# First feed-forward's gate and up products with seven block products for eight, on one Trainium2 core

## The chip, the cores and the metric

The program runs on one core of one Trainium2 chip. The metric is the device time of one execution in microseconds (us). The kernel before takes 1785.22 us, the median of three runs (1783.51 to 1785.93).

## What is computed

A block of two layers acts on 512 latent tokens and 256 context tokens of width 1024. Each layer normalizes and modulates its input, mixes the tokens (layer 0: neighbourhood attention and a convolution; layer 1: an mLSTM), and then runs a gated feed-forward of hidden width 2816. Layer 0 does this for all 768 tokens, layer 1 for the 512 latent ones only. The part that matters here:

```python
def swiglu(h, w_gate, w_up, w_down):
    return (jax.nn.silu(h @ w_gate) * (h @ w_up)) @ w_down
...
x = x + g2 * swiglu(modulate(x, norm_ffn_g[l], sh2, sc2), ffn_w_gate[l], ffn_w_up[l], ffn_w_down[l])
if not last:
    ctx = ctx + cg1 * out_ctx
    ctx = ctx + cg2 * swiglu(modulate(ctx, norm_ffn_g[l], csh2, csc2), ffn_w_gate[l], ffn_w_up[l], ffn_w_down[l])
```

The modulation vectors of both layers are products of a conditioning vector with a large matrix (`ada_w`, 96 tiles of 128 columns); 48 of these tiles, those of layer 1, are computed inside the first feed-forward.

## The kernel before

Activations lie feature-major: `X`, `h_hi` and `h_lo` are 128 partitions x 8 tiles x 768 tokens. To keep fp32 accuracy at the pace of the faster fp32r format, each operand is split in two parts, a high part (rounded to fp32r, by a copy on ScalarE) and a low part (the rest, by a subtraction on VectorE). A product of weights and activations is then three matmuls per tile of the contraction: high x high, high x low, low x high.

**One weight chunk** is a row of `in_w`: 128 partitions x 1024 numbers, that is 8 contraction tiles for 128 output features. SyncE loads it into `raw[j]` (j is 0 or 1, its loop is at L377 to L383), as soon as VectorE has finished with the chunk that lay there. ScalarE copies it to `w_hi[j]` (`split_hi`, L452), which waits until the product that last used `w_hi[j]` is done; VectorE subtracts to `w_lo[j]` (`split_lo`, L457). `product` (L471) runs on TensorE:

```python
for w, m in ((w_hi, m_hi), (w_hi, m_lo), (w_lo, m_hi)):
    n += 1
    for a, b in cols:
        last = nc.tensor.matmul(G[j][:, a:b], w[:, j, k], m[:, k, a:b], ...)
```

In the first feed-forward `cols` is `BOTH`, so each weight tile is used by a matmul of 512 columns and one of 256; in the second it is `ONLY`, 512 columns. `G[0]` is PSUM banks 0 and 1, `G[1]` banks 2 and 3.

**The feed-forward** takes its 22 hidden tiles in `GROUPS` of 8, 8 and 6 (the third item of the pair is the count). For each tile a gate product goes to `G[0]` and an up product to `G[1]`. ScalarE applies SiLU to the gate (L607, to `sg`), VectorE multiplies with the up product (L1162, to `ftmp`), ScalarE copies to `c_hi` (L610), VectorE subtracts to `c_lo` (L1164). After a group come eight down products, one for each tile of the 1024 output features, over the 8 or 6 hidden tiles of the group; their last contraction tile waits for the last hidden tile. VectorE adds each into `X` (`residual`, L1150, two instructions of 512 and 256 columns). The first pair of products is written so that each contraction tile is used as soon as the norm has made it (L1716).

**Conditioning tiles.** Between the down products of the first feed-forward stands one round of conditioning work for every two down products, 12 rounds of 4 tiles. ScalarE issues four transfers of 512 KB each (L618), TensorE multiplies them after the even down product (L1725, 64 recorded matmuls a round), ScalarE copies the rows (L622), TensorE folds them after the odd one (L1732), VectorE adds the bias (L1171). In the last group each `residual` is followed by the squares for the next norm (L578, L1105).

The order on each engine is the order in which it is written; all engines run their own in-order queue and wait on semaphores. GpSimd only makes attention masks in layer 0 (L413 to L418) and small products in layer 1 (L443); it is idle during both feed-forwards.

## Time and profile before

| | before |
|---|---|
| median of three runs | 1785.22 us |
| the profiled execution's own time | 1781.29 us |
| its span, first to last instruction | 1779.5 us |
| TensorE busy | 1694.7 us, 95% of the span |
| VectorE busy | 802.9 us, 45% |
| ScalarE busy | 592.7 us, 33% |
| GpSimd busy | 68.0 us, 4% |
| granted TensorE clock, mean | 0.983 |
| first feed-forward | about 444 to 1038 us |
| second feed-forward | about 1405 to 1771 us |

The profile is one execution, recorded by the hardware. An engine's busy time counts its instructions, and matmuls overlap in it, so that the pace of TensorE is read from how often something repeats rather than from one matmul's length. An instruction that others wait for is named as the releaser of their idle time. The granted clock of TensorE is 1.00 at 2.4 GHz and 0.50 at 1.2 GHz.

### The profile page before, as it was taken

To read this page: it belongs to the slowest core of one execution; us is meant where nothing else is said; L and a number is where in the kernel's file an instruction comes from. 1 tells how busy PE (TensorE), PEld (TensorE's weight loads), DVE (VectorE), ACT (ScalarE), POOL (GpSimd) and SP (SyncE) were. 2 spreads that over 40 slices of the span, in tenths; PEclk is the share of its full clock that TensorE was granted. 3 is DMA by queue.
4 is the path that set the end of the run, shared out by engine and by line. 5 is a ranking of instruction groups with operands and counts; after the bars stand their busy time and mean duration, and the time that the engine had idled before them with its cause. 6 is when DMAs were issued, how large, how long until landed. Compare 5 with 4: busy or idle time off the path is not lost.

```text
span 1779.5 us, 26603 instructions
## 1 busy us (share of the span) xinstructions
PE 1694.7 (95%) x10524; PEld 1404.3 (79%) x10524; DVE 802.9 (45%) x1192; ACT 592.7 (33%) x1021; POOL 68.0 (4%) x116
## 2 busy tenths in 40 slices
PE   5999999888999999999999988999998899999998
PEld 4888877677888888888888866777776688888886
DVE  5787776534422222222222355666644533333333
ACT  4344444442322112221122232455564422222221
POOL 0321011000000000000000000000000000000000
PEclk9999999899999999999999998999999999999999
DMA  8713333211112532124212531111113232233223
GB/s 333 108 48 120 128 110 119 82 34 62 48 59 63 197 106 59 61 97 165 102 60 91 183 130 39 46 36 36 48 48 107 71 105 95 94 94 106 94 95 118
DMA packets 47219, 168.99 MB, mean 95 GB/s; under 512 B 5296, under 2 KB 5552, under 8 KB 47024
## 3 DMA queue, kind: packets, MB, share of 16 engines
q1 hardware_dynamic: 31408, 115.47, 20.1%
q10 hardware_dynamic: 14976, 51.52, 7.9%
q0 software_dynamic: 768, 1.08, 0.8%
...
## 4 chain that ended last, share of the span: by engine, by line
PE 89%; DVE 3%; ACT 3%; DMA 2%; issue 1%; SPq 0%; ACTq 0%; DVEq 0%
PE PS L471 53%; PE PS L1839 9%; PE PS L2027 7%; PE PS L1716 3%; DMA scr<-in_ada 2%; PE PS L1725 2%; PE PS L1882 2%; PE PS L1898 1%; PE PS L2115 1%; PE PS L1732 1%; PE PS L2114 1%; DVE c_early L1466 1%; PE PS L1778 1%; PE PS L1864 1%; PE PS L1982 1%
## 5 line engine op out<-in xcount | busy, mean ns | idle before, releaser
L457 DVE TENSOR_TENSOR w_lo<-raw,w_hi 128x1024 fp32r<-128x1024 f32 x196 | 239.8, 1224 | 253.2 <-ACT w_hi L452 247.3
L471 PE MATMUL PS<-h_hi,w_hi 128*128 128x512 f32 x1008 | 302.2, 354 | 2.5 <-DVE w_lo L457 2.5
L471 PE MATMUL PS<-h_hi,w_lo 128*128 128x512 f32 x1008 | 301.8, 353 | 0.0
L471 PE MATMUL PS<-h_lo,w_hi 128*128 128x512 f32 x1008 | 301.8, 353 | 0.0
L452 ACT ACTIVATE w_hi<-raw 128x1024 fp32r<-128x1024 f32 x196 | 206.5, 1054 | 261.3 <-PE PS L471 217.9
L471 PE MATMUL PS<-c_hi,w_hi 128*128 128x512 f32 (+1 forms) x672 | 203.5, 357 | 4.7 <-DVE w_lo L457 4.7
L471 PE MATMUL PS<-c_lo,w_hi 128*128 128x512 f32 (+1 forms) x672 | 201.5, 354 | 0.0
L471 PE MATMUL PS<-c_hi,w_lo 128*128 128x512 f32 (+1 forms) x672 | 201.4, 354 | 0.0
L471 PEld LDWEIGHTS PS<-h_hi,w_hi 128*128 128x128 f32 x1008 | 165.1, 188 | 30.5 <-DVE w_lo L457 3.3
L471 PEld LDWEIGHTS PS<-h_hi,w_lo 128*128 128x128 f32 x1008 | 165.2, 188 | 27.5
L471 PEld LDWEIGHTS PS<-h_lo,w_hi 128*128 128x128 f32 x1008 | 165.2, 188 | 27.5
L1150 DVE SCALAR_TENSOR_TENSOR X<-PS,mod,X 128x512 f32 (+1 forms) x96 | 60.6, 659 | 256.3 <-PE PS L471 240.1
L471 PEld LDWEIGHTS PS<-c_hi,w_hi 128*128 128x128 f32 x672 | 109.9, 188 | 25.5 <-DVE w_lo L457 5.6
L1284 DVE SCALAR_TENSOR_TENSOR c_early<-X,small,c_early 128x798 f32<-128x798 f32 x120 | 126.0, 1050 | 2.9
L471 PEld LDWEIGHTS PS<-c_hi,w_lo 128*128 128x128 f32 x672 | 110.2, 188 | 18.7
L471 PEld LDWEIGHTS PS<-c_lo,w_hi 128*128 128x128 f32 x672 | 110.1, 188 | 18.4
L610 ACT ACTIVATE c_hi<-scr 128x768 f32 (+3 forms) x44 | 32.6, 742 | 266.5 <-DVE scr L1162 266.5
L1162 DVE TENSOR_TENSOR scr<-PS,scr 128x768 f32<-128x768 f32 (+1 forms) x44 | 36.3, 825 | 169.6 <-PE PS L471 169.6
L2027 PE MATMUL PS<-h_hi,w_hi 128*128 128x512 f32 (+1 forms) x264 | 85.5, 378 | 12.8 <-ACT c_early L944 9.4
L607 ACT ACTIVATE scr<-PS 128x768 f32<-128x768 f32 (+1 forms) x44 | 31.1, 707 | 190.4 <-PE PS L471 184.6
L2027 PE MATMUL PS<-h_hi,w_lo 128*128 128x512 f32 (+1 forms) x264 | 81.0, 361 | 0.0
L2027 PE MATMUL PS<-h_lo,w_hi 128*128 128x512 f32 (+1 forms) x264 | 80.6, 360 | 0.0
...
## 6 DMA issues: line engine op xcount, KB each, us to landing
raw<-in_w SPq DMA_DIRECT2D x196, 512.0 KB, 3.5
...
scr<-in_ada SPq DMA_DIRECT2D x4, 1024.0 KB, 14.6
...
```

The lines of the kernel that those rows point to most:

```text
L452: nc.scalar.activation(w_hi[:, j], raw[:, j].rearrange("p (k n) -> p k n", k=KT), ACT.Copy).then_inc(s_hi, 1)
L457: nc.vector.tensor_tensor(w_lo[:, j], raw[:, j].rearrange("p (k n) -> p k n", k=KT), w_hi[:, j].bitcast(f32), ALU.subtract).then_inc(s_lo, 1)
L471: last = nc.tensor.matmul(G[j][:, a:b], w[:, j, k], m[:, k, a:b], start=(n == 1), stop=(n == 3 * k_tiles))
L610: nc.scalar.activation(c_hi[:, bass.ds(i, 1), 0:cols].rearrange("p a n -> p (a n)"), ftmp[:, 0:cols], ACT.Copy).then_inc(s_hhi, 1)
L1150: i = V.scalar_tensor_tensor(out=xs, in0=G[j][:, a:b], scalar=gv, in1=xs, op0=ALU.mult, op1=ALU.add)
L1162: V.tensor_tensor(ftmp[:, 0:cols], G[1][:, 0:cols], sg[:, 0:cols], ALU.mult).then_inc(s_gf[1], 1)
L1284: V.scalar_tensor_tensor(out=y, in0=src, scalar=w, in1=y, op0=ALU.mult, op1=ALU.add)\
L1716: last = MM(G[j][:, a:b], x[:, j, k], m[:, k, a:b], start=(k == 0 and n == 0), stop=(k == KT - 1 and n == 2))
L1725: last = MM(PS[g:g + 32, bank, 128 * q:128 * q + 128], sT[:, k], w[:, 128 * k:128 * k + 128], start=(k < 4), stop=(k >= 4))
L1839: last = MM(dst[:, a:b], w[:, p % 2, k], m[:, k, a:b], start=(k == 0 and n == 0), stop=(k == KT - 1 and n == 2))
L1882: last = MM(PS[0:size, 6 + h, 128 * n:128 * n + 128], Pb[:, U % 2, h, c:c + size], dg[:, U % 2, h], start=True, stop=True)
L2027: last = MM(dst[:, a:b], w[:, i % 2, k], m[:, k, a:b], start=(k == 0 and n == 0), stop=(k == KT - 1 and n == 2))
```

## The change

**The block product.** In the first feed-forward, 20 of the 22 hidden tiles are no longer computed by a gate and an up product over 768 tokens. The weights of a pair (gate tile and up tile) and the activations are cut in two halves of the contraction (4 tiles each) and the tokens in two halves of 384 (`HALF`). Of the 2 x 2 block product, Strassen's scheme (in Winograd's form) needs seven products of blocks in place of eight: `block(q, b)` for pair `q`, `b` from 0 to 6, each of 4 contraction tiles x 3 matmuls of 384 columns, into PSUM bank `BLOCK_BANK[b]`. The first two hidden tiles (`PLAIN`) stay as they were.

**Weight sums.** With a0, a1 the two halves of the gate tile and u0, u1 those of the up tile, blocks 1, 4, 2 and 6 take a0 - u0, u0 + u1, u0 + u1 - a0 and a1 - (u0 + u1 - a0). GpSimd makes them (`weight_sum`, four 128 x 512 operations a pair), mostly in place in the loaded chunks. Each block's weights are then split as before, now in pieces of 512 numbers (`block_hi` on ScalarE, `block_lo` on VectorE), into five slots: the four halves of `w_hi`/`w_lo` and `slot4`. Slots 2 and 3 are used twice a pair (`BLOCK_SLOT`).

**Activation sums.** Once, at the start: GpSimd and VectorE add high and low parts of the four blocks of `h` back together (`whole`, two each, 128 x 1536), VectorE forms four differences (`h_sum`), ScalarE and VectorE split them (`sum_hi`, `sum_lo`, four each). One of them is put over a part of `h_hi`/`h_lo`, and waits for the last plain product to have read it (`s_b12`).

**After the blocks.** ScalarE copies block 0's result to SBUF (`p1s`), VectorE forms seven sums of PSUM blocks with 384-column intermediates (`sums`, `gate0`, `up1`, `up0`, `gate1`); SiLU and the multiplication with it are each done in two halves; `c_hi` and `c_lo` are made as before.

**Groups.** `GROUPS` is 6, 6, 6 and 4 hidden tiles, in both feed-forwards, so that there are 32 down products in each instead of 24, over the same 22 hidden tiles. The conditioning work of the first feed-forward is 16 rounds of 3 tiles. Both weight buffers `raw` and `adaw` carry the gate and up chunks of alternate pairs, and conditioning tiles go to `adaw` and a piece of `scr`. The code of the first feed-forward is written out (`ffn_first`) where there were loops; the second (`ffn`) keeps its loops.

```diff
 GD_END = 20
-GROUPS = ((0, 8), (8, 8), (16, 6))
+GROUPS = ((0, 6), (6, 6), (12, 6), (18, 4))
+PLAIN = 2
+PAIRS = tuple(f0 + nf - PLAIN for f0, nf in GROUPS)
+FIRST = (0,) + PAIRS[:-1]
 GRID = 64
...
+        SUMS = [[tw[:, x, y] for y in range(2)] for x in range(2)] + [[h_hi[:, 0:4, HALF:T], h_lo[:, 0:4, HALF:T]]]
+        SUMS += [[v[:, 6:8].rearrange("p a (b n) -> p (a b) n", b=2) for v in (c_hi, c_lo)]]
+        SUM_RAW = (four(tw_raw[:, 0, 1]), four(tw_raw[:, 1, 1]), b12, four(c_early[:, 1, 6 * T:8 * T]))
+        B11, B21, B22 = ([x[:, a:a + 4, b:b + HALF] for x in (h_hi, h_lo)] for a, b in ((0, 0), (4, 0), (4, HALF)))
+        MOVING = (B11, SUMS[2], SUMS[1], B21, SUMS[0], SUMS[3], B22)
+        SLOTS = [[x[:, j, a:a + 4] for x in (w_hi, w_lo)] for j in range(2) for a in (0, 4)]
+        SLOTS += [[slot4[:, 0], slot4[:, 1]]]
+        BLOCK_SLOT = (0, 1, 2, 3, 4, 2, 3)
+        BLOCK_BANK = (0, 1, 2, 3, 5, 6, 7)
...
+        def slot_free(engine, q, b):
+            g = FIRST.index(q) if q in FIRST else None
+            if b >= 5:
+                engine.wait_ge(s_bp, 7 * q + b - 2)
+            elif g is None:
+                engine.wait_ge(s_bp, 7 * (q - 1) + (1, 2, 6, 7, 5)[b])
+            elif b < 4:
+                engine.wait_ge(s_gemm, R_F0 + 2 * PLAIN + 8 * g - (b < 2))
+            else:
+                engine.wait_ge(s_adm, 48 + 12 * g)
...
+            R = R_F0 + 2 * PLAIN
+            for g in range(len(GROUPS)):
+                for q in range(FIRST[g], PAIRS[g]):
+                    for c in range(2):
+                        if q == FIRST[g]:
+                            sp.wait_ge(s_lo, R - 1 + c)
+                        elif q == 1:
+                            sp.wait_ge(s_adm, 48)
+                        elif q == FIRST[g] + 1:
+                            sp.wait_ge(s_adm, 48 + 12 * g)
+                        else:
+                            sp.wait_ge(s_bl, 7 * (q - 1))
+                        sp.dma_start(chunk(q, c), A["w"][R + 2 * q + c]).then_inc(s_pw[q % 2][c], 16)
...
+            def weight_sum(q, i):
+                a0, a1, u0, u1 = (four(chunk(q, c)[:, n:n + 512]) for c in range(2) for n in (0, 512))
+                if i == 0:
+                    slot_free(pool, q, 1)
+                    for c in range(2):
+                        pool.wait_ge(s_pw[q % 2][c], 16 * (q // 2) + 16)
+                    dst, x, y, op = block_raw(q, 1), a0, u0, ALU.subtract
+                elif i == 1:
+                    pool.wait_ge(s_sb, 4 * q + 1)
+                    dst, x, y, op = u0, u0, u1, ALU.add
+                elif i == 2:
+                    pool.wait_ge(s_sb, 4 * q + 2)
+                    pool.wait_ge(s_bl, 7 * q + 1)
+                    dst, x, y, op = a0, u0, a0, ALU.subtract
+                else:
+                    pool.wait_ge(s_sb, 4 * q + 3)
+                    pool.wait_ge(s_bl, 7 * q + 4)
+                    dst, x, y, op = a1, a1, a0, ALU.subtract
+                nc.gpsimd.tensor_tensor(dst, x, y, op).then_inc(s_sb, 1)
...
+        def block_hi(act, q, b):
+            slot_free(act, q, b)
+            if b in (0, 3, 5):
+                act.wait_ge(s_pw[q % 2][b == 5], 16 * (q // 2) + 16)
+            else:
+                act.wait_ge(s_sb, 4 * q + {1: 1, 4: 2, 2: 3, 6: 4}[b])
+            nc.scalar.activation(SLOTS[BLOCK_SLOT[b]][0], block_raw(q, b), ACT.Copy).then_inc(s_bh, 1)
+        def block_lo(dve, q, b):
+            hi, lo = SLOTS[BLOCK_SLOT[b]]
+            dve.wait_ge(s_bh, 7 * q + b + 1)
+            nc.vector.tensor_tensor(lo, block_raw(q, b), hi.bitcast(f32), ALU.subtract).then_inc(s_bl, 1)
...
+                        last = q + 1 == PAIRS[g]
+                        block_hi(act, q, 2)
+                        if q > FIRST[g]:
+                            second_half_silu(q - 1)
+                        act.wait_ge(s_bp, 7 * q + 1)
+                        act.wait_ge(s_g0, q)
+                        nc.scalar.activation(p1s, partial(0), ACT.Copy).then_inc(s_sn, 1)
+                        block_hi(act, q, 3)
+                        if q == 0:
+                            act.wait_ge(s_gf[1], half + 1)
+                            hidden_hi(1)
+                        elif q > FIRST[g]:
+                            pair_hi(q - 1, q + 1 - f0)
+                        block_hi(act, q, 4)
+                        block_hi(act, q, 5)
+                        block_hi(act, q, 6)
+                        first_half_silu(q)
+                        if not last:
+                            block_hi(act, q + 1, 0)
+                            block_hi(act, q + 1, 1)
+                    act.wait_ge(s_bp, 7 * q + 2)
+                    split_hi(act, R // 2, 0)
+                    act.wait_ge(s_bl, 7 * q + 7)
+                    act.wait_ge(s_bp, 7 * q + 5)
+                    ada_next(4 * g)
+                    second_half_silu(q)
+                    pair_hi(q, q + 2 - f0)
...
+                def sums(q):
+                    dve.wait_ge(s_bp, 7 * q + 3)
+                    dve.wait_ge(s_sn, q + 1)
+                    dve.wait_ge(s_u4, q)
+                    V.tensor_tensor(u2s, partial(2), p1s, ALU.add).then_inc(s_u2, 1)
+                    dve.wait_ge(s_u2, q + 1)
+                    dve.wait_ge(s_u0, q)
+                    V.tensor_tensor(u3s, partial(1), u2s, ALU.add).then_inc(s_u3, 1)
+                def gate0(q):
+                    dve.wait_ge(s_bp, 7 * q + 4)
+                    if q:
+                        dve.wait_ge(s_f, 2 * q - 1)
+                    else:
+                        dve.wait_ge(s_gf[1], half + 1)
+                    V.tensor_tensor(sg[:, 0:HALF], partial(3), p1s, ALU.add).then_inc(s_g0, 1)
+                def up1(q):
+                    dve.wait_ge(s_bp, 7 * q + 5)
+                    dve.wait_ge(s_g1s, q)
+                    V.tensor_tensor(u4s, partial(4), u2s, ALU.add).then_inc(s_u4, 1)
+                    dve.wait_ge(s_u3, q + 1)
+                    dve.wait_ge(s_hid, q + PLAIN)
+                    V.tensor_tensor(ftmp[:, HALF:T], partial(4), u3s, ALU.add).then_inc(s_u1, 1)
+                def up0(q):
+                    dve.wait_ge(s_bp, 7 * q + 6)
+                    V.tensor_tensor(ftmp[:, 0:HALF], partial(5), u3s, ALU.add).then_inc(s_u0, 1)
...
+                dve.wait_ge(s_h, 16)
+                whole(b12, h_hi[:, 0:4, HALF:T], h_lo[:, 0:4, HALF:T])
+                split_lo(dve, half, 0)
+                whole(b22, *B22)
+                gated(half - 1)
+                dve.wait_ge(s_ty, 1)
+                dve.wait_ge(s_tz, 1)
+                h_sum(SUM_RAW[0], b12, b11)
+                hidden_lo(0, 0)
+                split_lo(dve, half, 1)
+                dve.wait_ge(s_ty, 2)
+                dve.wait_ge(s_ts, 1)
+                h_sum(SUM_RAW[2], b22, b12)
+                h_sum(SUM_RAW[1], b22, SUM_RAW[0])
+                dve.wait_ge(s_tz, 2)
+                dve.wait_ge(s_ts, 3)
+                h_sum(SUM_RAW[3], b21, SUM_RAW[1])
+                block_lo(dve, 0, 0)
+                sum_lo(2)
+                block_lo(dve, 0, 1)
+                sum_lo(1)
+                gated(half)
...
+                        if q > FIRST[g]:
+                            gate1(q - 1)
+                        block_lo(dve, q, 2)
+                        if q > FIRST[g]:
+                            gated1(q - 1)
+                        if q == 0:
+                            sum_lo(0)
+                        block_lo(dve, q, 3)
+                        if q == 0:
+                            hidden_lo(1, 1)
+                            sum_lo(3)
+                        elif q > FIRST[g]:
+                            hidden_lo(q + 1, q + 1 - f0)
+                        block_lo(dve, q, 4)
+                        sums(q)
+                        block_lo(dve, q, 5)
+                        gate0(q)
+                        block_lo(dve, q, 6)
+                        up1(q)
+                        if not last:
+                            block_lo(dve, q + 1, 0)
+                        else:
+                            split_lo(dve, R // 2, 0)
+                        up0(q)
+                        gated0(q)
+                        if not last:
+                            block_lo(dve, q + 1, 1)
+                    gate1(q)
+                    gated1(q)
+                    hidden_lo(q + 2, q + 2 - f0)
...
+            def block(q, b):
+                g = FIRST.index(q) if q in FIRST else None
+                pe.wait_ge(s_bl, 7 * q + b + 1)
+                if q:
+                    pe.wait_ge((s_sn, s_u3, s_u2, s_g0, s_u1, s_u0, s_g1s)[b], q)
+                if g is not None and b in (0, 2):
+                    pe.wait_ge(s_gf[b // 2], R_F0 // 2 + PLAIN + 4 * g)
+                if g and b == 4:
+                    pe.wait_ge(s_mod, 20 + 4 * g)
+                if q == 0 and b in (1, 2, 4, 5):
+                    pe.wait_ge(s_tl[{1: 2, 2: 1, 4: 0, 5: 3}[b]], 1)
+                (w_h, w_l), (m_h, m_l) = SLOTS[BLOCK_SLOT[b]], MOVING[b]
+                for k in range(4):
+                    for n, (x, m) in enumerate(((w_h, m_h), (w_h, m_l), (w_l, m_h))):
+                        last = MM(partial(b), x[:, k], m[:, k], start=(k == 0 and n == 0), stop=(k == 3 and n == 2))
+                last.then_inc(s_bp, 1)
```

**VectorE, one pair of the first feed-forward.** `L457` was `split_lo`; now `L602` is `block_lo`, `L1410` to `L1443` are the sums over PSUM, `L1449` and `L1455` the multiplications with the SiLU, `L1403` makes `c_lo`. Before, the body of the loop:

```order
L457 TENSOR_TENSOR w_lo<-raw,w_hi 128x1024
L456 ISA
L457 TENSOR_TENSOR w_lo<-raw,w_hi 128x1024
L1162 TENSOR_TENSOR scr<-PS,scr 128x768
L1163 REGISTER_ALU
L1164 ISA
L1164 TENSOR_TENSOR c_lo<-scr,c_hi 128x768
```

Now, a pair within a group, from the sums of its first blocks on (the two rows at the end belong to the next pair's block 1 and to the last sum of this one):

```order
L1410 TENSOR_TENSOR scr<-PS,scr 128x384
L1413 TENSOR_TENSOR scr<-PS,scr 128x384
L602 TENSOR_TENSOR w_lo<-raw,w_hi 128x512
L1422 TENSOR_TENSOR scr<-PS,scr 128x384
L602 TENSOR_TENSOR w_lo<-raw,w_hi 128x512
L1428 TENSOR_TENSOR scr<-PS,scr 128x384
L1431 TENSOR_TENSOR scr<-PS,scr 128x384
L602 TENSOR_TENSOR w_lo<-adaw,w_hi 128x512
L1436 TENSOR_TENSOR scr<-PS,scr 128x384
L1449 TENSOR_TENSOR scr<-scr 128x384
L602 TENSOR_TENSOR w_lo<-w_early,w_hi 128x512
L1443 TENSOR_TENSOR scr<-PS,scr 128x384
```

Four operations a pair became 17, the weight parts of the next block standing between the sums of the last.

**VectorE, between the norm and the first block.** `L586` is now `split_lo`, `L1398` the plain multiplication, `L1388` an `h_sum`, `L1393` a `sum_lo`. Before, only `split_lo`, L1162 and L1164 stood there. Now, from the first plain multiplication to the low part of block 1:

```order
L1398 TENSOR_TENSOR scr<-PS,scr 128x768
L1388 TENSOR_TENSOR scr<-c_early 128x1536
L1403 TENSOR_TENSOR c_lo<-scr,c_hi 128x768
L586 TENSOR_TENSOR w_lo<-raw,w_hi 128x1024
L1388 TENSOR_TENSOR c_early<-c_early 128x1536
L1388 TENSOR_TENSOR scr<-c_early,scr 128x1536
L1388 TENSOR_TENSOR c_early<-c_early,scr 128x1536
L602 TENSOR_TENSOR w_lo<-raw,w_hi 128x512
L1393 TENSOR_TENSOR h_lo<-c_early,h_hi 128x4x384
L602 TENSOR_TENSOR w_lo<-w_early,w_hi 128x512
```

Six operations of 1536 elements stand here that were not there before.

**GpSimd.** Before, no instruction stood between the last mask of layer 0 and layer 1. Now:

```order
L518 AFFINE_SELECT c_early<-X 128x64
L527 TENSOR_TENSOR c_early<-h_hi,h_lo 128x1536 x2
L548 TENSOR_TENSOR w_early<-raw 128x512
L548 TENSOR_TENSOR raw<-raw 128x512 x3
L548 TENSOR_TENSOR w_early<-adaw 128x512
L548 TENSOR_TENSOR adaw<-adaw 128x512 x3
```

The last four rows repeat ten times, for 20 pairs.

## Rows read from the trace of the kernel before

**Rows 1.** The page's parts 1 and 2: busy share of each engine, and the granted clock
```profile
PE 1694.7 (95%) x10524; PEld 1404.3 (79%) x10524; DVE 802.9 (45%) x1192; ACT 592.7 (33%) x1021; POOL 68.0 (4%) x116
...
PEclk9999999899999999999999998999999999999999
```

**Rows 2.** Windows of TensorE: stretch, its length, PE busy (xinstructions), granted clock, DMA share, GB/s
```profile
478.00:981.00 503.00, 501.60 (x3369) 1.00 0.28 98
```

**Rows 3.** Timeline of VectorE, first feed-forward (start, us, engine, line, operation, idle before)
```profile
481.63 0.96 DVE L1162 TENSOR_TENSOR scr<-PS,scr 128x768 f32<-128x768 f32 x1 [5.37 <-PE PS L471]
...
581.48 0.96 DVE L1162 TENSOR_TENSOR scr<-PS,scr 128x768 f32<-128x768 f32 x1 [5.37 <-PE PS L471]
```

**Rows 4.** Timeline of VectorE, second feed-forward
```profile
1433.69 0.69 DVE L1162 TENSOR_TENSOR scr<-PS,scr 128x512 f32<-128x512 f32 x1 [2.71 <-PE PS L471]
...
1498.97 0.69 DVE L1162 TENSOR_TENSOR scr<-PS,scr 128x512 f32<-128x512 f32 x1 [2.70 <-PE PS L471]
```

**Rows 5.** Timeline of TensorE inside one product: matmuls of 512 and 256 columns, weight loads
```profile
584.21 0.31 PEld L471 LDWEIGHTS PS<-c_hi,w_hi 128*128 128x128 f32 x2
584.32 0.51 PE L471 MATMUL PS<-c_hi,w_hi 128*128 128x512 f32 x2
```

**Rows 6.** Groups by line and form, VectorE and ScalarE: xcount, busy us, mean ns of one
```profile
L457 DVE TENSOR_TENSOR w_lo<-raw,w_hi 128x1024 fp32r<-128x1024 f32 x196 | 239.8, 1224 | 253.2 <-ACT w_hi L452 247.3
...
L1162 DVE TENSOR_TENSOR scr<-PS,scr 128x768 f32<-128x768 f32 x22 | 21.1, 958 | 112.8 <-PE PS L471 112.8
...
L1162 DVE TENSOR_TENSOR scr<-PS,scr 128x512 f32<-128x512 f32 x22 | 15.2, 692 | 56.8 <-PE PS L471 56.8
...
L610 ACT ACTIVATE c_hi<-scr 128x768 f32 x21 | 17.8, 849 | 162.0 <-DVE scr L1162 162.0
...
L610 ACT ACTIVATE c_hi<-scr 128x512 f32 x21 | 13.3, 634 | 100.4 <-DVE scr L1162 100.4
```

**Rows 7.** Groups by line and form, GpSimd
```profile
L443 POOL TENSOR_TENSOR scr<-scr,const 48x512 f32<-48x512 f32 x16 | 16.7, 1042 | 227.2 <-PE PS L2099 198.7 <-DVE scr L1618 28.6
```

**Rows 8.** Timeline of VectorE and GpSimd, first mixer; then one line of VectorE: ns min/median/max
```profile
155.55 1.22 DVE L457 TENSOR_TENSOR w_lo<-raw,w_hi 128x1024 fp32r<-128x1024 f32 x1
155.58 1.33 POOL L415 TENSOR_SCALAR_AFFINE_SELECT scr<-X 128x64 f32<-128x64 f32 x1 [51.85 <-DVE scr L1318]
...
L1284 DVE SCALAR_TENSOR_TENSOR c_early<-X,small,c_early x120: 1035/1050/1087, 62.1 to 305.6; 128x798 f32<-128x798 f32 x120
```

**Rows 9.** Timeline of VectorE, then TensorE, where the first feed-forward begins
```profile
457.53 0.48 DVE L1118 SCALAR_TENSOR_TENSOR h_lo<-scr,mod,h_hi 128x256 fp32r<-128x256 f32 x1
...
463.33 1.23 DVE L457 TENSOR_TENSOR w_lo<-raw,w_hi 128x1024 fp32r<-128x1024 f32 x1 [5.33 <-ACT w_hi L452]
...
464.62 0.61 PE L471 MATMUL PS<-h_hi,w_hi 128*128 128x512 f32 x2 [0.99 <-DVE w_lo L457]
```

**Rows 10.** Timeline of TensorE after a long idle, and the window behind it
```profile
444.17 0.98 PE L1716 MATMUL PS<-h_hi,w_hi 128*128 128x512 f32 x2 [5.54 <-DVE h_lo L1118]
...
444.00:449.00 5.00, 4.83 (x15) 0.50 0.00 0
```

**Rows 11.** Timeline of VectorE and TensorE, down products; what TensorE waited for before L1725
```profile
600.52 1.14 DVE L1150 SCALAR_TENSOR_TENSOR X<-PS,mod,X 128x512 f32 x2 [8.27 <-PE PS L471]
...
620.14 1.14 DVE L1150 SCALAR_TENSOR_TENSOR X<-PS,mod,X 128x512 f32 x2 [8.13 <-PE PS L471]
...
589.62 1.95 PE L1725 MATMUL PS<-scr,sT 128*32 128x128 f32 x64
...
  DMA scr<-in_ada: 8.2, 13
```

**Rows 12.** Timeline of VectorE, last group of the second feed-forward, and its weight transfers
```profile
1738.33 0.69 DVE L1162 TENSOR_TENSOR scr<-PS,scr 128x512 f32<-128x512 f32 x1 [2.70 <-PE PS L471]
1739.93 0.69 DVE L1164 TENSOR_TENSOR c_lo<-scr,c_hi 128x512 f32 x1 [0.91 <-ACT c_hi L610]
...
DMA to landing us min/median/max: 3.4/3.5/3.6
```

410 lines of the change are left out of this document (276 added, 134 removed).

## The prediction

> **What bounds the kernel now.** I read the page's busy shares first. TensorE is busy 95% of the span at a granted clock near 1.0, every other engine under half [rows 1]. In the window that holds nearly all of the first feed-forward, 503.0 us long, TensorE has work for 501.60 us at a granted clock of 1.00 [rows 2]. So in this stage no wait ends last: only fewer or shorter matmuls can shorten it, provided that the others keep up.
>
> The pace comes from a repeat. From one plain multiplication of a pair to the next but five lie six periods, 99.85 us, so a pair (48 times 512 + 256 columns) takes 16.64 us [rows 3]. In the second feed-forward six periods take 65.28 us, so 48 matmuls of 512 columns take 10.88 us, 226.7 ns each [rows 4]. The remaining 16.64 - 10.88 = 5.76 us are 48 matmuls of 256 columns, 120.0 ns each. The difference, 106.7 ns for 256 columns, is 2.4 GHz; a matmul costs its columns plus 13.3 ns.
>
> **What the change removes.** By that line a matmul of 384 columns takes 160.0 + 13.3 = 173.3 ns. A pair of the new kind has 7 x 4 x 3 = 84 of them: 14.56 us. Against 16.64 us this is 2.08 us less, and for 20 pairs **-41.6 us**. The interpolation rests on the weight load staying hidden. One load is recorded as 188 ns or so (two take 0.31 us, starting 0.12 us apart), but the 512-column matmul behind it starts 0.11 us after the load [rows 5], and a 256-column matmul leaves it only 120 ns. 173 ns is more room than that.
>
> **What the other engines must now do in 14.56 us.** VectorE's 128x512 and 128x768 operations take 0.692 and 0.958 us, so 1.04 ns an element, and 0.559 us for 384. ScalarE's take 0.634 and 0.849 us, and 0.527 us for 384 [rows 6]. A pair needs on VectorE 7 low parts (4.84), 7 sums and 2 multiplications (5.03) and one `c_lo` (0.96): 10.8 us. On ScalarE 7 high parts (4.44), one copy and two SiLUs (1.58), one `c_hi` (0.85): 6.9 us. GpSimd needs four sums; the nearest row is its 48x512 operation of 1.042 us [rows 7], so 4.2 us.
>
> Totals below 14.56 are not enough: each block needs its weights in time. I walk VectorE's queue from the start of block 0, 2.08 us a block, with 0.25 us from a block's end to its reader and 0.1 us for a handover (my readings). The two sums after block 2 (end 6.24) are done at 7.7, the low part for block 5 at 8.4; it is due at 10.40. `gate0` after block 3, then block 6's low part at 9.9; due 12.48. `up1`, then the next block 0's at 12.5; due 14.56. `up0`, the multiplication, then the next block 1's at 14.6; due 16.64. `gate1`, then block 2's at 16.1; due 18.72. Block 3's high part stands behind ScalarE's copy of block 0: low part 18.8, due 20.80. `c_lo` and block 4's: 20.6, due 22.88. **The spare is never under 2.0 us.** The PSUM banks are read a whole pair ahead. The chunk for a pair is asked for when the pair two before it is split, some 9 us ahead of the first sum of it; a transfer takes 3.5 us [rows 12]. I cost all this at nothing, with 1.5 us in total for stalls of single blocks; its cover is those 2.0 us.
>
> **GpSimd against VectorE.** One thing can use up the spare. A GpSimd operation on 64 columns that started 0.03 us after a `w_lo` lasted 1.33 us, to just behind VectorE's end. VectorE's own accumulations next to GpSimd's masks stayed between 1035 and 1087 ns in 120 cases [rows 8]. So GpSimd waits for VectorE; whether VectorE waits for GpSimd the trace does not show, since GpSimd's masks are short. Bounds: 0, or four times 1.042 us a pair. I take a value between, since both do not meet each time and sums that read PSUM ran beside GpSimd. VectorE then has 10.8 to 15.0 us of work, likely about 13, under 14.56.
>
> The Trainium skill ("SBUF — State Buffer", section "SBUF: two separate sides") says the pair of ports that VectorE and GpSimd share is an exclusive lock, taken for a whole instruction when VectorE has two SBUF inputs and GpSimd reads SBUF, and that the second to start blocks. By that rule the trace agrees for GpSimd waiting; VectorE waiting would be my first rival below.
>
> **The start.** The last `h_lo` ends at 458.0 us; TensorE's second pair waited for its first low part until 464.6 [rows 9]. New before that low part: one 1536-element operation on VectorE (0.958 + 768 x 1.04 ns = 1.76 us) and two on GpSimd (3 x 1.042 = 3.1 us each at most). If all three stand in line, the part is ready at 458.0 + 1.8 + 6.3 + 1.2 = 467.3, 2.7 us late; if GpSimd never holds VectorE, nothing is late. Then VectorE has 1.76 us nine times more (one `whole`, four `h_sum`, four `sum_lo`), 15.8 us, besides its usual work, until the first pair's middle, 25 us later. In my walk the low part for block 4 of pair 0 comes about 1 us late, and with GpSimd's first sums between 3 us late. A wait also can cost clock: after 5.54 us idle, TensorE ran 4.83 us at 0.50 of its clock [rows 10], 2.4 us lost. Bounds 0 and 9 us; I take **+5**, the middle, since all the queues are crowded there.
>
> **More rounds and groups.** Two down products with a round take 620.14 - 600.52 = 19.62 us, against 16.64 without: 2.98 us a round, 35.8 us for 12. Of this 1.95 us are 64 row matmuls [rows 11], for three tiles 0.27 + 47 x 0.0267 = 1.5 us; the rest scaled gives about 0.8. So 16 x 2.35 = 37.6 us: **+2**. Bounds: 16 rounds at three quarters, 0; 16 unshortened rounds, +11.9. TensorE waited 8.2 us for conditioning transfers [rows 11], mostly in the last group, where ScalarE asks for them behind the squares. There products shrink from 6.24 to 4.16 us, but only three rounds instead of four wait, for three tiles instead of four: I take no change, bounds -4 and +4.
>
> A group's last hidden tile must be ready before the last contraction tile of its first down product. Its path is now 0.25 + 0.56 + 0.53 + 0.56 + 0.85 + 0.96 us and four handovers, 4.1 us. With six tiles that matmul starts 5.2 us after the blocks: covered by the five tiles ahead. With four it starts at 9 x 0.3467 = 3.1 us: **+1**. In the second feed-forward `c_lo` ends 1740.62, 2.5 us after the up product (the multiplication at 1738.33 began 0.25 us behind it) [rows 12], against 9 x 0.2267 = 2.0 us: +0.5. There a weight chunk also is the longer cycle in the group of four: transfer 3.5, high 1.05, low 1.23, handovers 0.25, 6.0 us for two products that take 5.44; three times over, +1.7. Together **+2.2**. The eight more evictions and splits of each feed-forward are covered elsewhere, since six tiles give products of 6.24 and 4.08 us against 1.23 + 1.1 us of VectorE. The code is written out where it looped; the mixers run written-out code now at the same pace, so nothing.
>
> **Sum.** -41.6 + 1.5 + 5 + 2 + 0 + 1 + 2.2 = -29.9 us. Against the profiled execution's 1781.29 us this gives 1751.4; that run stood 3.9 us below the median of the three runs, 1785.22, against which I predict **1755.3 us**. Within this case the ends give about 1746 to 1769.
>
> **Rivals.** (1) GpSimd holds VectorE for each whole sum. VectorE's pair is then 10.8 + 4.2 = 15.0 us, up to 15.8 with gaps that its waits for blocks leave, and it sets the pace: 20 x 0.44 to 20 x 1.24, +9 to +25 us, about 1772. For it: the 1.33 us row shows that one engine can wait for the other's instruction. Against: it would need nearly every sum to collide. Chance 0.13.
>
> (2) Slower: GpSimd's sums on 128 partitions with two plain inputs are much longer than the 48-partition row, and hold VectorE. The gain of 41.6 less 11.7 of costs leaves 29.9 us, 1.5 us a pair, so the change loses once a pair passes 16.1 us; with VectorE at 10.8 + 4s this is s = 1.3 us. At twice the row, 2.08 us, a pair takes 19.2 us, +92 us: about 1848. Against: the operation works on partitions side by side, and the row's 512 elements are the same. Chance 0.06.
>
> (3) The weight load does set the pace, because a single matmul of 384 columns now stands behind each load: 84 x 0.188 = 15.8 us a pair, +24.6 us, about 1780. Against: the 256-column matmuls at 120 ns. Chance 0.04.
>
> The forecast has 0.77. Range, with the start and GpSimd wide: **1746 to 1776**. A measurement here can tell about 0.2%, 3.6 us. Faster by more than that 0.90, within it 0.03, slower 0.07: the forecast and nearly all of (1) and (3) are faster, (2) and a tail of (1) are not.
>
> **What would show it.** TensorE's blocks at 173 ns a matmul and 14.56 us from one `gate0` to the next, with next to no wait for `block_lo`. GpSimd's sums near 1.04 us, longer only where they start inside a VectorE instruction. VectorE's 512-element low parts at 0.69 us; at up to 1.7 us they would show (1). A wait of TensorE of a few microseconds near the second plain pair and in pair 0. In the last groups, short waits before the last contraction tile. I am wrong if a pair's period is over 15 us, or if the start costs over 9 us.

## The result, and the profile after

The changed kernel takes 1762.16 us (median of 4 runs, 1759.95 to 1766.52), beside 1785.58 us (4 runs, 1783.51 to 1787.18) for the kernel before: ratio 0.9876, 95% interval 0.9854 to 0.9898. The prediction was 1755.3 us, range 1746 to 1776. The profiled execution took 1763.85 us with a span of 1761.7 us, 17.8 us under the span of before.

The page, busy time by engine and granted clock by slice (compare [rows 1]):

```profile
PE 1666.7 (95%) x10284; PEld 1410.9 (80%) x10284; DVE 1008.5 (57%) x1506; ACT 668.3 (38%) x1185; POOL 211.7 (12%) x198
...
PEclk8999999999999999999999988999999999999999
```

TensorE still sets the time. It is busy 28 us less and the span is only 17.8 us shorter, so some 10 us of new idle time must be somewhere. I cut the span where TensorE's rows change their operands (the first row of a stage to the first row of the next); the last column is the difference.

| stretch | before, us | after, us | difference |
|---|---|---|---|
| last plain pair ahead of the first block | one pair, 16.65 | 18.09 | +1.4 |
| 20 pairs | 20 of 21 pairs in 349.72: 333.1 | 65.26 + 87.76 + 87.76 + 58.54 = 299.3 | -33.8 |
| down stages of the first feed-forward | 78.58 + 78.41 + 75.43 = 232.4 | 3 x 59.92 + 60.93 = 240.7 | +8.3 |
| mixer to second feed-forward | 361.2 | 364.4 | +3.2 |
| second feed-forward | 363.0 | 366.2 | +3.2 |

The five differences add up to -17.7; the rest of the execution is the same to 0.2 us. Windows of the changed kernel (stretch, length, busy us of PE, PEld, DVE, ACT and POOL with instructions, granted clock, DMA share, GB/s): the groups' pairs, then a down stage and the last one.

```profile
482.57:547.83 65.26, 61.08 (x339) 59.91 (x337) 54.06 (x71) 24.28 (x42) 24.99 (x14) 0.97 0.19 65
607.75:695.51 87.76, 87.76 (x507) 87.76 (x507) 67.65 (x101) 35.61 (x63) 33.99 (x21) 1.00 0.21 72
...
903.11:961.65 58.54, 58.54 (x338) 58.54 (x338) 44.26 (x67) 23.17 (x41) 20.73 (x13) 1.00 0.20 72
547.83:607.75 59.92, 59.92 (x505) 51.66 (x505) 21.29 (x30) 12.19 (x16) 4.53 (x3) 1.00 0.50 176
...
961.65:1015.42 53.77, 47.68 (x413) 38.45 (x412) 28.02 (x39) 20.66 (x25) 0.00 (x0) 0.97 0.56 190
```

Six pairs take 87.76 us, 14.63 us each, 84 matmuls of 174.1 ns; TensorE has no gap in them. The first four need 65.26 us, 6.7 us more than four times 14.63, with 4.2 us of TensorE's time idle. VectorE has 67.65 / 6 = 11.3 us a pair, GpSimd 5.7, ScalarE 5.9. Of the 6.7 us, 4.2 are waits for VectorE, and most of the rest is a lower granted clock behind the longest of them. The timeline of TensorE (the first two rows belong to the plain pair ahead, the others to pair 0):

```profile
464.48 0.61 PE L615 MATMUL PS<-h_hi,w_hi 128*128 128x512 f32 x2 [1.12 <-DVE w_lo L586]
...
473.99 0.61 PE L615 MATMUL PS<-h_hi,w_hi 128*128 128x512 f32 x2 [0.92 <-DVE w_lo L586]
...
485.37 0.44 PE L2112 MATMUL PS<-h_hi,w_hi 128*128 128x384 f32 x1 [0.52 <-DVE w_lo L602]
...
488.51 0.62 PE L2112 MATMUL PS<-h_sums,w_hi 128*128 128x384 f32 x2 [0.75 <-DVE w_lo L602]
...
496.08 3.63 PE L2112 MATMUL PS<-h_sums,slot 128*128 128x384 f32 x12 [2.91 <-DVE slot L602]
```

Behind the wait of 2.91 us, 12 matmuls take 3.63 us where 12 x 0.174 = 2.1 would do, at a granted clock of 0.60 (window, columns as above):

```profile
496.08:500.37 4.29, 4.29 (x16) 4.29 (x17) 3.29 (x7) 1.56 (x3) 1.09 (x1) 0.60 0.13 23
```

The timelines of VectorE and GpSimd over the same time show what VectorE was doing:

```profile
464.34 5.06 DVE L1384 TENSOR_TENSOR c_early<-h_hi,h_lo 128x1536 f32<-128x1536 f32 x1
...
480.77 2.85 DVE L1393 TENSOR_TENSOR h_lo<-c_early,h_hi 128x1536 fp32r<-128x1536 f32 x1
...
491.51 2.84 DVE L1393 TENSOR_TENSOR c_lo<-c_early,c_hi 128x1536 fp32r<-128x1536 f32 x1
...
494.28 1.75 DVE L602 TENSOR_TENSOR slot<-raw,slot 128x512 fp32r<-128x512 f32 x1
```

```profile
458.24 9.54 POOL L527 TENSOR_TENSOR c_early<-h_hi,h_lo 128x1536 f32<-128x1536 f32 x2 [153.49 <-DVE h_lo L1342]
...
490.87 1.88 POOL L548 TENSOR_TENSOR raw<-raw 128x512 f32<-128x512 f32 x1 [6.10 <-DVE w_lo L602]
```

Other operations on 1536 elements take VectorE 1.75 us, low parts of 512 elements 0.69 us. The longest ends its own length behind the end of a GpSimd operation: at 464.34 + 5.06 = 469.40, beside 458.24 + 9.54 = 467.78 and 1.75 us of its own; so does the one at 491.51, beside GpSimd's end at 492.75. (From the first plain multiplication to block 1's low part stand five operations of 1536 elements, not six as the section on the change counts.) The same holds inside the pairs. VectorE's groups by form from 607.75 to 695.5 us (xcount, busy us, mean ns, idle before):

```profile
L602 DVE TENSOR_TENSOR w_lo<-adaw,w_hi 128x512 fp32r<-128x512 f32 x15 | 10.8, 720 | 4.6 <-ACT w_hi L596 4.3
L602 DVE TENSOR_TENSOR slot<-adaw,slot 128x512 fp32r<-128x512 f32 x3 | 5.4, 1784 | 0.0
...
L602 DVE TENSOR_TENSOR slot<-raw,slot 128x512 fp32r<-128x512 f32 x3 | 4.2, 1417 | 0.0
...
L1449 DVE TENSOR_TENSOR scr<-scr 128x384 f32<-128x384 f32 x6 | 4.2, 699 | 0.6
...
L1410 DVE TENSOR_TENSOR scr<-PS,scr 128x384 f32<-128x384 f32 x6 | 3.3, 547 | 1.9 <-PE PS L2112 1.9
```

The low part of block 4 always meets the next pair's weight sum and takes 1.4 to 1.8 us; sums that read PSUM keep 0.55 us. GpSimd's sums take 1.6 us in the mean, not 1.04:

```profile
L548 POOL TENSOR_TENSOR adaw<-adaw 128x512 f32<-128x512 f32 x9 | 14.5, 1606 | 25.1 <-DVE w_lo L602 24.9
L548 POOL TENSOR_TENSOR raw<-raw 128x512 f32<-128x512 f32 x7 | 11.5, 1638 | 23.9 <-DVE w_lo L602 23.7
```

In the last down stage TensorE waits for conditioning transfers. Waits of TensorE from 440 to 1100 us (total us, times, longest):

```profile
PE PS L2087 <- DMA adaw<-in_ada: 2.7, 5, 1.0
PE PS L2087 <- DMA scr<-in_ada: 2.6, 3, 1.2
```

That is 5.3 us, all in the last down stage, beside 3.0 us in the kernel before.

### The profile page after: what moved, and what is told of

It reads as the page before. It is cut to its first block, busy times and chain, and to the rows that moved or that the text cites. A ratio compares the mean times of both kernels' runs of the same rounds, so it can differ in the third digit from the quotient of the medians.

```text
span 1761.7 us, 26390 instructions
## 1 busy us (share of the span) xinstructions
PE 1666.7 (95%) x10284; PEld 1410.9 (80%) x10284; DVE 1008.5 (57%) x1506; ACT 668.3 (38%) x1185; POOL 211.7 (12%) x198
## 4 chain that ended last, share of the span: by engine, by line
PE 86%; DVE 5%; ACT 4%; DMA 3%; issue 1%; SPq 0%; ACTq 0%; DVEq 0%
PE PS L615 33%; PE PS L2112 16%; PE PS L2235 9%; PE PS L2423 7%; PE PS L2078 3%; PE PS L2087 3%; PE PS L2278 2%; DMA scr<-in_ada 2%; PE PS L2294 1%; PE PS L2511 1%; PE PS L2510 1%; PE PS L2094 1%; PE PS L2378 1%; PE PS L2174 1%; PE PS L2260 1%
## 5 line engine op out<-in xcount | busy, mean ns | idle before, releaser
L586 DVE TENSOR_TENSOR w_lo<-raw,w_hi 128x1024 fp32r<-128x1024 f32 x172 | 210.6, 1225 | 120.3 <-ACT w_hi L581 114.0
L1374 DVE SCALAR_TENSOR_TENSOR X<-PS,mod,X 128x512 f32<-128x512 f32 (+1 forms) x120 | 75.7, 659 | 226.4 <-PE PS L615 210.0
L615 PE MATMUL PS<-h_hi,w_hi 128*128 128x512 f32 x368 | 139.2, 385 | 3.6 <-DVE w_lo L586 3.6
L615 PE MATMUL PS<-h_hi,w_lo 128*128 128x512 f32 x368 | 139.0, 385 | 0.0
L615 PE MATMUL PS<-h_lo,w_hi 128*128 128x512 f32 x368 | 138.9, 384 | 0.0
L2112 PE MATMUL PS<-h_hi,w_hi 128*128 128x384 f32 x320 | 107.5, 336 | 0.5 <-DVE w_lo L602 0.5
L2112 PE MATMUL PS<-h_lo,w_hi 128*128 128x384 f32 x320 | 107.0, 335 | 0.0
L2112 PE MATMUL PS<-h_hi,w_lo 128*128 128x384 f32 x320 | 107.0, 334 | 0.0
L615 PEld LDWEIGHTS PS<-h_hi,w_hi 128*128 128x128 f32 x368 | 68.0, 188 | 18.5 <-DVE w_lo L586 4.6
L615 PEld LDWEIGHTS PS<-h_lo,w_hi 128*128 128x128 f32 x368 | 67.9, 188 | 13.8
L615 PEld LDWEIGHTS PS<-h_hi,w_lo 128*128 128x128 f32 x368 | 68.0, 188 | 13.6
```

The lines of the kernel that those rows point to most:

```text
L586: nc.vector.tensor_tensor(w_lo[:, j], raw[:, j].rearrange("p (k n) -> p k n", k=KT), w_hi[:, j].bitcast(f32), ALU.subtract).then_inc(s_lo, 1)
L1374: i = V.scalar_tensor_tensor(out=xs, in0=G[j][:, a:b], scalar=gv, in1=xs, op0=ALU.mult, op1=ALU.add)
L2112: last = MM(partial(b), x[:, k], m[:, k], start=(k == 0 and n == 0), stop=(k == 3 and n == 2))
```

## The experiments

Theory: the pairs are worth 40 us and TensorE paces them; VectorE and GpSimd exclude each other in both directions, which is hidden behind TensorE in the steady pairs and costs only at the start; the rest of the loss is the regrouping. Rivals: GpSimd's sums hold the pairs up, the down stages are slow because of the block products' traffic, the start is VectorE's own work.

**The regrouping alone.** The kernel before, with

```diff
-GROUPS = ((0, 8), (8, 8), (16, 6))
+GROUPS = ((0, 6), (6, 6), (12, 6), (18, 4))
-                    for q in range(4):      # four conditioning tiles a round, 12 rounds
+                    for q in range(3):      # three, 16 rounds
```

> The kernel before with the regrouping alone: both feed-forwards in groups of 6, 6, 6 and 4 tiles, three conditioning tiles a round in 16 rounds, all products plain, nothing on GpSimd. Theory A (the regrouping costs, the block products give): the rounds of the first feed-forward cost about 4 us more than before, its last down stage about 5 us (transfers of the conditioning weights that the stage of four tiles is too short for), the second feed-forward about 3 us: 12 us in all, 1797.5 us, ratio 1.007, and the block products by themselves give 35 us. Rival B (the down stages are slow because GpSimd's sums and the other transfers of the block products disturb them): the regrouping costs under 4 us, at most 1789.5 us, and the stage of four tiles takes the same 19.6 us per two products as the stage of six tiles before.

Measured: 1806.57 us, ratio 1.0136 (1.0101 to 1.0170), twice what theory A gave. By stages against before: down stages +11.3 us, second feed-forward +3.5 us, mixer +1.5 us, all near theory A but for the first, and **+6.8 us in the plain pairs, whose code is unchanged**. Rival B falls: the regrouping alone costs the down stages more than theory A gave them. In the plain pairs TensorE has no gap and its granted clock is 1.00. Timelines of TensorE, two rows that lie 48 rows apart, first of the kernel before, then of this one:

```profile
465.06 0.52 PE L471 MATMUL PS<-h_lo,w_hi 128*128 128x512 f32 x2
...
481.71 0.51 PE L471 MATMUL PS<-h_lo,w_hi 128*128 128x512 f32 x2
```

```profile
465.06 0.51 PE L471 MATMUL PS<-h_lo,w_hi 128*128 128x512 f32 x2
...
482.01 0.51 PE L471 MATMUL PS<-h_lo,w_hi 128*128 128x512 f32 x2
```

A row is one matmul of 512 and one of 256 columns. They follow each other in 16.65 / 48 = 346.9 ns in the one and 16.95 / 48 = 353.1 ns in the other. In the first feed-forwards of all the traces nearly all uninterrupted stretches of such rows lie at 346.7 or at 353.3 ns (within 1 ns), and nearly all keep their rhythm from one interruption to the next. The kernel before has 346.7 in all its pairs but the first, and 353.3 in five of its 24 down products (96 of 528 rows). This kernel has 353.3 in nearly every stretch: 17.0 us a pair, and in the down products 432 rows more than before x 6.6 ns = 2.9 us.

The changed kernel has 353.3 in its down stages too, from the second product on, in about 370 rows more than the kernel before. So of its +8.3 us there, 2.4 us are this rhythm. A down stage of six tiles takes 59.92 us, of which 18 rows x 0.3467 + 126 x 0.3533 = 50.8 us are the products; 2.29 us are left for each of its four rounds, 36.6 us for 16. In the kernel before the same sum, 78.42 - 192 x 0.3467 = 11.85 us for four rounds, gives 35.5 us for 12. So the rounds cost 1.1 us, and the last stage the other 4.8. This last figure is no fixed one: in this trace and the seven others of kernels with the same last stage, the stage takes 58.8 to 64.2 us. The pairs of matmuls of 384 columns keep 174.1 ns each.

**Is the rhythm drawn anew in each execution?** Two kernels: the first feed-forward alone regrouped, and the kernel before once more.

```diff
-                for g, (f0, nf) in enumerate(GROUPS):
+                for g, (f0, nf) in enumerate((GROUPS, GROUPS1)[layer]):   # GROUPS1: 8, 8, 6
```

> The kernel before with the regrouping of its first feed-forward alone (6, 6, 6 and 4 tiles, three conditioning tiles a round); the second keeps 8, 8 and 6. In the earlier run with both regrouped, TensorE's rows of two matmuls (512 and 256 columns) were 353.3 ns apart from 450 to 1055 us, in the kernel before 346.7 ns, though the code of a pair is the same: that made 6.8 us in the pairs and 3.5 us in the down products. Theory A (regrouping costs 1 us in the rounds and 5 to 6 us in the last down stage, and the rhythm of 353.3 ns comes with it again): 17.0 us a pair, the kernel 20 us over the one before, ratio 1.011. Theory B (the rhythm of a stretch is drawn anew in each execution): stretches at 346.7 and at 353.3 ns mixed, pairs of 16.65 us in some of them, ratio 1.004 to 1.008.

> The kernel before once more, for a second trace of it. Theory A (the rhythm belongs to the kernel): rows of two matmuls 346.7 ns apart in the first feed-forward, pairs of 16.65 us, as in its first trace. Theory B (drawn anew in each execution): some stretches of it at 353.3 ns, pairs there of 16.97 us.

Measured: ratio 1.0098 (1.0077 to 1.0120) and 353.3 ns throughout, six pairs in 101.85 us; the kernel before again 346.7 ns, eight pairs in 133.21 us. Windows of the two, in this order:

```profile
612.24:714.09 101.85, 101.85 (x578) 88.28 (x578) 24.80 (x25) 20.22 (x23) 0.00 (x0) 1.00 0.20 62
```

```profile
658.54:791.75 133.21, 133.21 (x770) 116.50 (x770) 33.16 (x33) 27.10 (x31) 0.00 (x0) 1.00 0.19 63
```

Theory A holds for the first feed-forward's plain pairs: two traces of the kernel before agree, and so do the two regrouped kernels; the second trace of the kernel before differs from the first in which of its down products have 353.3. All ten traces of kernels with block products have 353.3 in the down stages, from the second product of each on, but for short pieces in the last stage. Elsewhere it does change from one execution to the next: the one plain pair before the block products ran at 346.7 up to its wait in the first trace of the changed kernel and at 353.3 in the second. What sets it was not found. Against the regrouped plain kernel (1.0136) the block products are worth 2.6% of the kernel before, 46 us; some 6 of them (960 rows x 6.6 ns) are the slower rhythm in that kernel's 20 pairs.

**The conditioning transfers of the last down stage, issued one product earlier.**

```diff
+                        if g < 3 and o and o % 2 == 0:
-                        if o and o % 2 == 0:
                             ada_next(4 * g + o // 2)
...
                         if g == 3:
+                            if o % 2 and o < 7:
+                                ada_next(4 * g + o // 2 + 1)
```

> The changed kernel with one thing moved: in the last down stage of the first feed-forward ACT issues the next three transfers of conditioning weights right behind the copy that ends a round, one product earlier than now. Theory A (TensorE waits there for these transfers, about 5 us in all): the last down stage falls from 53.6 to about 49 us, 1757.5 us for the kernel, 4 to 5 us under the changed one. Rival B (the transfers share their time with the weight transfers, whose sum is what the stage waits for; earlier issue only moves the wait): under 1 us gained.

Measured: ratio 0.9837 (0.9810 to 0.9864), 1754.00 us beside 1781.45 for before; TensorE's waits for these transfers are gone, and the last down stage with the norm behind it takes 52.72 instead of 60.93 us. Windows of its products alone, of the changed kernel and of this one:

```profile
961.65:1013.30 51.65, 45.71 (x406) 37.36 (x405) 25.95 (x36) 18.76 (x23) 0.00 (x0) 0.97 0.58 197
```

```profile
963.26:1006.70 43.44, 42.89 (x406) 36.53 (x405) 26.12 (x36) 18.09 (x23) 0.00 (x0) 1.00 0.65 224
```

TensorE's idle time falls from 5.9 to 0.6 us, its busy time for the same 406 matmuls by 2.8 us, with the granted clock from 0.97 to 1.00: behind the second round's waits, 12 rows had taken 5.65 us, 471 ns each instead of 353. Theory A holds, and the gain is larger than its 4 to 5 us. Rival B falls, although the transfers did get slower (median 5.7 and 7.1 us to landing, from 4.4 and 5.7): they now have the time.

**The second feed-forward in groups of 8, 8 and 6.**

```diff
-                for g, (f0, nf) in enumerate(GROUPS):
+                for g, (f0, nf) in enumerate(GROUPS1):      # in the second feed-forward: 8, 8, 6
```

> The changed kernel with the second feed-forward back in groups of 8, 8 and 6 tiles, the first as changed. Theory A (one more round of residuals and a last group of only four tiles cost 3 us there): the second feed-forward takes 363.0 us as before instead of 366.2, 1759 us for the kernel. Rival B (its extra time comes from elsewhere, from order or alignment of the transfers after the mixers): under 1 us gained.

Measured: the second feed-forward took 363.1 us, 3.1 us less, as theory A said. The whole is less clear: 0.9868 (0.9836 to 0.9900), which contains the ratio without the edit.

**All four additions of 1536 columns on VectorE.**

```diff
-            for dst, (hi, lo) in ((b11, B11), (b21, B21)):
-                nc.gpsimd.tensor_tensor(dst, hi.bitcast(f32), lo.bitcast(f32), ALU.add).then_inc(s_tz, 1)
                 whole(b12, h_hi[:, 0:4, HALF:T], h_lo[:, 0:4, HALF:T])
+                whole(b11, *B11)
                 split_lo(dve, half, 0)
-                whole(b22, *B22)
                 gated(half - 1)
+                whole(b22, *B22)
...
+                whole(b21, *B21)
```

> The changed kernel with the two additions of 1536 columns that GpSimd does at the start of the first feed-forward (9.54 us for the two) moved to VectorE, where the other two stand; GpSimd then does nothing until the weight sums. Theory A (GpSimd and VectorE exclude each other while both read two operands from SBUF, and VectorE's addition of 5.06 us at 464.34 is one of 1.76 us that waits for GpSimd): all four additions take about 1.8 us each on VectorE, the waits of 2.9 us and less before block (0, 2) and its neighbours shrink, and the start costs 2 to 4 us less than in the changed kernel, 1759 us. Rival B (no exclusion, the 5.06 us are the operation's own reads): VectorE has two more operations of 3.4 us in pair 0, the first blocks wait longer, and the kernel is 2 to 5 us slower than the changed one, 1765 us or more.

Measured: the additions on VectorE take 1.75 us each,

```profile
459.41 3.43 DVE L1380 TENSOR_TENSOR c_early<-h_hi,h_lo 128x1536 f32<-128x1536 f32 x2
...
465.75 1.75 DVE L1380 TENSOR_TENSOR c_early<-h_hi,h_lo 128x1536 f32<-128x1536 f32 x1
```

and from the feed-forward's first row to its first down product it takes 101.1 instead of 103.5 us: -2.4 us, as theory A said of the start. VectorE spends 6.9 us on four of them, as much as on two beside GpSimd (1.76 + 5.06 us): the 3.3 us of the long one were waiting. But the wait of 2.9 us in pair 0 stayed as it was, and the ratio 0.9892 (0.9861 to 0.9922) doesn't tell the kernel from the changed one.

**More, other and less work on GpSimd.** Behind (or instead of) its 80 weight sums:

```diff
                 nc.gpsimd.tensor_tensor(dst, x, y, op).then_inc(s_sb, 1)
+                # first:  one more sum of 128x512, const + const
+                # second: two memsets of 128x512
-                # third:  for i > 0 the sum on [:, :, 0:1] alone
```

> The changed kernel with one more addition of 128x512 on GpSimd behind each of its 80 weight sums (two operands from the constants in SBUF, the result never read). Theory A (VectorE and GpSimd exclude each other while both read SBUF): GpSimd has 8 instead of 4 operations in a pair, VectorE's three low parts with two SBUF operands that meet one grow from 0.69 to 1.4 us and more, VectorE's busy time in six pairs rises from 67.4 us by 6 to 25 us, while the sums that read PSUM keep their 0.55 us; the pair stays at 14.6 us as long as VectorE is under that, at most 15.5 us: 0 to 18 us for the kernel. Rival B (no exclusion, only GpSimd itself is slower beside VectorE): VectorE's durations and the pair's 14.6 us stay as they are.

> The same dose as the one before in another form: behind each weight sum two memsets of 128x512 on GpSimd, which read nothing. Theory A (exclusion by what both read): VectorE's low parts keep their present mix of about 0.7 us and, beside a weight sum, 1.4 to 1.8 us, VectorE's busy time in six pairs stays within 2 us of 67.4, the pair at 14.6 us. Rival B (any GpSimd work beside VectorE costs it): busy time rises as it does with the sums.

> The changed kernel with three of GpSimd's four weight sums of each pair cut to one column in four places (it leaves out their other columns, so the block weights are other ones). Theory A (TensorE's matmuls pace the pair, the exclusion is hidden): the pair stays at 14.6 us, VectorE's low parts that wait for GpSimd now (0.79 to 1.78 us) fall to 0.7 us, VectorE's busy time in six pairs from 67.4 us by 4 to 8 us, the kernel within 0.2% of the changed one outside pair 0. Rival B (the weight sums hold the pairs up in waits too short to be seen): the pair falls by 0.05 us or more, to 14.56 us.

The third leaves out most columns of three of the four sums, so its results are other ones. One execution of each: 1769.36, 1761.39 and 1757.62 us, beside 1780.99 for before. Windows of the first group of six pairs, in this order (compare 607.75 to 695.51 of the changed kernel above):

```profile
609.66:700.01 90.35, 89.30 (x506) 87.42 (x506) 81.24 (x101) 35.58 (x63) 68.80 (x43) 1.00 0.20 70
```

```profile
605.05:692.81 87.76, 87.76 (x506) 87.76 (x506) 69.33 (x101) 35.73 (x63) 53.40 (x63) 1.00 0.20 72
```

```profile
601.46:689.21 87.75, 87.75 (x506) 87.75 (x506) 60.20 (x101) 35.56 (x63) 15.28 (x21) 1.00 0.20 73
```

VectorE does the same operations in all four, in 60.2 us with narrow sums, 67.7 with the kernel's own, 69.3 with memsets added and 81.2 with sums added. So 42 memsets (22.1 us of GpSimd) cost it 1.7 us, 22 added sums 13.6 us, 0.6 us each. By form, with narrow sums and with added sums:

```profile
L603 DVE TENSOR_TENSOR slot<-adaw,slot 128x512 fp32r<-128x512 f32 x3 | 2.1, 690 | 0.0
```

```profile
L608 DVE TENSOR_TENSOR w_lo<-w_early,w_hi 128x512 fp32r<-128x512 f32 x5 | 8.9, 1778 | 0.0
...
L1420 DVE TENSOR_TENSOR scr<-PS,scr 128x384 f32<-128x384 f32 x6 | 3.3, 558 | 0.2
```

VectorE's operations with two SBUF operands wait for GpSimd's, those that read PSUM don't. By "SBUF: two separate sides" of the Trainium skill's "SBUF — State Buffer" an operation blocks while the other engine reads SBUF through the ports they share; that is what the runs show. The same six pairs take 87.76 us with narrow sums and with the kernel's own: the kernel's conflicts are hidden behind TensorE, rival B falls. With added sums they show, 90.35 / 6 = 15.06 us a pair, and over the 20 pairs 14 waits for block 4's low part, four of them in these six.

The narrow sums tell what GpSimd costs at the start: the first four pairs take 60.39 instead of 65.26 us. **4.9 of their 6.7 us are GpSimd's weight sums**, the three of each pair that were cut, by their own length and by what they hold up: the low part of an activation sum at 479.33 there takes 1.75 us where it took 2.85, and so does the one at 487.88. The waits of 0.52 and 0.75 us are gone and the longest is 1.69 us:

```profile
491.36 2.36 PE L2113 MATMUL PS<-h_sums,slot 128*128 128x384 f32 x12 [1.69 <-DVE slot L603]
```

That is 2.5 us of waits. Most of the other half of the 4.9 us is the clock: the 12 matmuls behind this shorter wait take 2.36 us and the granted clock stays at 1.00.

**The order on VectorE in pair 0**, with the changed kernel again beside it.

```diff
                         if q == 0:
                             hidden_lo(1, 1)
-                            sum_lo(3)
...
                         block_lo(dve, q, 4)
+                        if q == 0:
+                            sum_lo(3)
                         sums(q)
```

> The changed kernel again, as it is, beside the two that follow, on their chip: 0.9876 of the kernel before, within its interval of 0.9854 to 0.9898.

> The changed kernel with VectorE's order in pair 0 changed at one place: the low part of activation sum 3, which block 5 is the first to need, stands behind the low part of block 4's weights instead of ahead of it. Theory A (TensorE's wait of 2.91 us there, and the stretch at half clock behind it, come from VectorE's order, not from GpSimd's sum): the wait falls to 1.3 us or less, the 12 matmuls behind it from 3.6 to about 2.3 us, the stretch from the first block to the first down product from 65.3 to about 62.5 us, the kernel 2 to 4 us under the changed one. Rival B (GpSimd's third weight sum ends too late anyway): the wait stays over 2 us. Rival C: block 5 waits instead for its low part, and nothing is won.

Measured on one chip: the changed kernel 0.9869 (0.9849 to 0.9889), this one 0.9867 (0.9845 to 0.9890). The timeline of TensorE in pair 0:

```profile
492.31 2.39 PE L2113 MATMUL PS<-h_sums,slot 128*128 128x384 f32 x12 [0.21 <-DVE slot L602]
...
496.74 0.45 PE L2113 MATMUL PS<-c_hi,w_hi 128*128 128x384 f32 x1 [2.05 <-DVE w_lo L602]
```

Rival C: the wait of 2.91 us went from block 4 to block 5, and the stretch took 64.89 instead of 65.26 us. In the changed kernel VectorE is busy without a gap from 463 to 499 us. This other order only moved the wait; fewer conflicts, with the narrow sums, did shorten it.

**The four edits together.**

> The changed kernel with four edits together: conditioning transfers of the last down stage issued a product earlier, second feed-forward in groups of 8, 8 and 6, the four additions of 1536 columns all on VectorE, the low part of activation sum 3 behind block 4's. From the stages measured so far: -8.2 us in the last down stage, -3.1 us in the second feed-forward, -2.4 us at the start of the first, -3 us from the order in pair 0, -16.7 us together: 1745 us, ratio to before about 0.978. Rival (the gains at the start overlap, and steps of the clock and of the matmul rhythm elsewhere blur the rest): -10 to -12 us, 1750 us.

Measured: 1749.71 us, ratio 0.9804 (0.9785 to 0.9824), on the chip where the changed kernel took 1762.40 us: 12.7 us better, near the rival's 10 to 12 us and at its 1750 us; theory's 16.7 us did not come. The last down stage took 52.70 us and the second feed-forward 363.08 us, as in the single runs:

```profile
956.52:1009.22 52.70, 46.39 (x417) 38.32 (x417) 32.06 (x47) 23.88 (x31) 0.00 (x0) 1.00 0.70 238
1370.04:1733.12 363.08, 361.54 (x1584) 298.41 (x1584) 137.11 (x146) 97.90 (x117) 0.00 (x0) 0.99 0.28 93
```

The start gave 2.7 us in all, not the 5.4 expected: the order in pair 0 added almost nothing to the additions' move.

## Why the prediction was right, and where its terms were off

The faster time came by the mechanism of the forecast. The total lies 6.9 us above 1755.3 us. The spans, with -17.7 us measured against -29.9 predicted, are further apart, 12 us, because the profiled execution of the kernel before was 4.3 us under its median and that of the changed kernel 1.7 us over. Of the 12 us, 3 are the mixers' own scatter (below), and the rest comes from the terms:

| term | predicted | measured |
|---|---|---|
| 20 pairs and stalls of single blocks | -41.6 + 1.5 | -40.5, no stalls |
| start | +5 (0 to 9) | +1.4 + 6.7 = +8.1 |
| rounds | +2 (0 to 11.9) | +1.1 |
| conditioning transfers, last down stage | 0 (-4 to +4) | +4.8, with a wait of 0.6 for `c_lo` |
| group of four in the first feed-forward | +1 | in the row above |
| rhythm of the down products | not in the sum | +2.4 |
| mixers | 0 | +3.2, but within the scatter: 360.8 to 366.9 us in the 14 traces |
| second feed-forward | +2.2 | +3.2 |

**Pairs.** The interpolated 173.3 ns a matmul was 174.1 ns. The walk through VectorE's queue block by block held: with VectorE at 11.3 us a pair, where 13 was called likely, TensorE has no gap in the six pairs. By operations VectorE was cheaper than I counted (10.0 us with narrow sums, not 10.8), GpSimd's sums dearer (1.6, not 1.04 us).

**GpSimd against VectorE.** Rival 1 had the mechanism right, VectorE does wait for GpSimd, and its outcome wrong: three of the four sums cost VectorE 7.5 us in six pairs, 1.2 us a pair, since only those of its operations that have both operands in SBUF meet them. It takes twice the sums to lengthen a pair (15.06 us). Rivals 2 and 3 fell with the period.

**The start** was 3 us dearer than the middle of my bounds. The `whole` additions on GpSimd took 4.8 us each, over the 3.1 us that I had called the most, and held a VectorE operation for 3.3 us. I saw the wait before block 4, and sized it right (2.91 us, "3 us late"), partly by luck: GpSimd's first sums are 1.2 us of it (1.69 us with narrow sums), not the 2 us that I gave them. What the middle of my bounds left too little room for were the waits before blocks 1 and 2 (0.52 and 0.75 us), the clock behind the long wait and 1.4 us in the plain pair ahead.

**Conditioning transfers** is the step that failed most: I let shorter products and smaller rounds cancel. They don't. ScalarE asks for a round's tiles at the start of an even product, and TensorE needs them at that product's end, now 4.2 us later instead of 6.2, and a transfer in that stage, next to those of the weights, takes 4.4 to 5.7 us from its issue (medians). Issuing them earlier gave back 8.2 us. I also read 8.2 us of waits out of [rows 11]: that figure adds the idle time of the weight loads (5.2 us) to that of the matmuls, and the matmuls alone waited 3.0 us.

**The rounds** cost 1.1 us where I said 2. That the down stages of six tiles also changed their rhythm was in no term; without the comparison of rows its 2.4 us would have been put down to the rounds.
